# Two transformer blocks in one fp32 kernel: earlier loads of the down weights, and a new order of the activation sums' low parts

## The reference, cut to what matters

```
def swiglu_ffn(x, w_gu, w_down):            # first block, layers 0 and 1
    g, u = jnp.split(x @ w_gu, 2, axis=-1)
    return (jax.nn.silu(g) * u) @ w_down

def conv_ffn(h, w_gate, w_up, conv_w, conv_b, w_down):   # second block
    g = causal_dwconv(h @ w_gate, conv_w, conv_b)        # 3 taps along the tokens
    return (jax.nn.silu(g) * (h @ w_up)) @ w_down
```

## Time and profile before

| what | value |
|---|---|
| median of 3 runs | 2450.75 us (2448.09 to 2450.96) |
| the profiled execution's own time | 2450.39 us |
| its span, first to last instruction | 2448.6 us |
| PE busy | 2371.0 us (97%) |
| DVE busy | 1603.1 us (65%) |
| ACT busy | 1044.6 us (43%) |
| mean granted PE clock | 0.987 of full speed |
| chain that ended last | PE 86%, DVE 7%, ACT 3%, issue 2%, DMA 1% |

### The profile page before, as it was taken

The page is one execution under the profiler, slowest core; times in us unless marked ns, Lnnn a source line. Parts: engine busy times, 40 slices in busy tenths (PEclk is TensorE's granted clock), DMA queues, the critical chain, the costliest instruction groups (busy, mean ns, idle before and its releaser), DMA issues.

```text
span 2448.6 us, 36911 instructions
## 1 busy us (share of the span) xinstructions
PE 2371.0 (97%) x14899; PEld 2057.2 (84%) x14899; DVE 1603.1 (65%) x2174; ACT 1044.6 (43%) x1385; POOL 320.0 (13%) x258
## 2 busy tenths in 40 slices
PE   7699999999999999999999999999899999999899
PEld 7688899988886789998878669899788878899887
DVE  8835877835537678775675646899534545789832
ACT  5422544523226544444233644456322344355622
POOL 6403000003003240000232021000131002000000
PEclk9899999999999999999999999999999999999999
DMA  2423333333232133323333213232332312333232
GB/s 57 96 99 102 88 104 104 93 90 104 94 104 56 40 103 88 106 83 94 95 95 111 69 35 104 78 108 66 109 100 88 98 58 70 90 108 105 84 86 90
DMA packets 328204, 217.57 MB, mean 89 GB/s; under 512 B 11060, under 2 KB 318922, under 8 KB 327978
## 3 DMA queue, kind: packets, MB, share of 16 engines
q1 hardware_dynamic: 322298, 208.46, 29.1%
q0 software_dynamic: 2384, 5.80, 1.0%
q10 hardware_dynamic: 3360, 1.02, 0.2%
HBM read 206.59 MB, written 2.10 MB: 85 GB/s over the span
## 4 chain that ended last, share of the span: by engine, by line
PE 86%; DVE 7%; ACT 3%; issue 2%; DMA 1%; SPq 1%; ACTq 0%; POOL 0%; DVEq 0%
PE psum L1339 9%; PE psum L1341 9%; PE psum L1340 9%; PE psum L1095 8%; PE psum L1097 8%; PE psum L1096 8%; PE psum L1308 3%; PE psum L1309 3%; PE psum L1310 3%; PE psum L1477 2%; PE psum L1479 2%; PE psum L1478 2%; DVE w_lo L2918 1%; DMA w_stage<-in_ffn_w_down_dram 1%; PE psum L1207 1%
## 5 line engine op out<-in xcount | busy, mean ns | idle before, releaser
L2028 ACT CAST w_hi<-w_stage 128x2048 fp32r<-128x2048 f32 x129 | 246.6, 1912 | 720.9 <-PE psum L1097 409.8
L2918 DVE TENSOR_TENSOR w_lo<-w_stage,w_hi 128x2048 fp32r<-128x2048 f32 x126 | 298.7, 2371 | 287.3 <-ACT w_hi L2028 287.2
L1339 PE MATMUL psum<-x_sum_hi,w_hi 128*128 128x256 f32 x1088 | 310.0, 285 | 7.3 <-DVE hidden_raw L2975 7.3
L1340 PE MATMUL psum<-x_sum_lo,w_hi 128*128 128x256 f32 x1088 | 309.5, 285 | 0.0
L1341 PE MATMUL psum<-x_sum_hi,w_lo 128*128 128x256 f32 x1088 | 309.5, 285 | 0.0
L2096 ACT CAST w_hi<-w_parts 128x1024 fp32r<-128x1024 f32 x204 | 213.0, 1048 | 192.3 <-PE psum L1341 111.2
L3046 DVE TENSOR_TENSOR w_lo<-w_parts,w_hi 128x1024 fp32r<-128x1024 f32 x204 | 248.4, 1220 | 57.0 <-ACT w_hi L2096 55.9
L1339 PE MATMUL psum<-x_hi,w_hi 128*128 128x256 f32 x816 | 231.5, 284 | 0.0
L1341 PE MATMUL psum<-x_hi,w_lo 128*128 128x256 f32 x816 | 231.4, 284 | 0.0
L1340 PE MATMUL psum<-x_lo,w_hi 128*128 128x256 f32 x816 | 231.4, 284 | 0.0
L1095 PE MATMUL psum<-hidden_raw_hi,w_hi 128*128 128x512 f32 x572 | 224.0, 392 | 1.4 <-DVE w_lo L2918 1.4
(11 more groups left out here) (586 smaller groups left out, 5330.2 us busy)
## 6 DMA issues: line engine op xcount, KB each, us to landing
w_stage<-in_ffn_w_down_dram SPq DMA_DIRECT2D x64, 704.0 KB, 4.6
w_parts<-in_ffn_w_gu_dram SPq DMA_DIRECT2D x144, 256.0 KB, 3.5
w_parts<-in_ffn_w_gate_dram SPq DMA_DIRECT2D x64, 256.0 KB, 3.1
w_parts<-in_ffn_w_up_dram SPq DMA_DIRECT2D x64, 256.0 KB, 3.0
w_stage<-in_sb_w_qkv_dram SPq DMA_DIRECT2D x12, 1024.0 KB, 5.2
w_stage<-in_od_w_in_dram SPq DMA_DIRECT2D x12, 1024.0 KB, 5.3
w_stage<-in_ev_w_in_dram SPq DMA_DIRECT2D x10, 1024.0 KB, 5.1
w_stage<-in_ssm_w_glu_dram SPq DMA_DIRECT2D x8, 1024.0 KB, 5.4
```

The costliest lines, as they stand in the source:

```text
L1339: nc.tensor.matmul(dst, hi, x_hi[:, k, :], start=(start and k == 0), stop=False, skip_group_check=True)
L1340: nc.tensor.matmul(dst, hi, x_lo[:, k, :], start=False, stop=False, skip_group_check=True)
L2028: nc.scalar.copy(whi[:, half, :], wst[:, half, :]).then_inc(whi_done, 1)
L2918: V.tensor_tensor(wlo[:, half, :], wst[:, half, :], whi[:, half, :].bitcast(F32), ALU.subtract).then_inc(wlo_done, 1)
```

## The change

Three things are changed. (1) On SP the first down weights and the rest of each half are loaded half by half: half 0 after product 3 of the last iteration, half 1 after product 7; the down loop then begins with its second column block (`first`). (2) The low parts of the activation sums get a semaphore of their own, `x_low`; PE no longer waits for all four at the start, and each product that uses a sum waits for as many as it needs. To have a semaphore for this, `gv_link` is dropped and `rstds_done` counts in its place. (3) In the conv stages DVE makes the low parts of T1 and T2 before the first seven-product iteration and those of T3 and T4, with the sums of four, inside it; the taps come ahead of the sums of two; ACT rounds T2 between the first and second activations of the last plain iteration. In the gu stages two of the four low parts trade places.

```diff
@@ SP, part_loads and the loop over stages
-                sp.wait_ge(product_done, products_count(name, SEVEN_ITERS[name] - 1, 9))
+                down = run[run.index(name) + 1]
                 for half in range(2):
+                    sp.wait_ge(product_done, products_count(name, SEVEN_ITERS[name] - 1, 3 + 4 * half))
+                    sp.dma_start(tile_view(wst, down, half), tile_source(down, 0, half)).then_inc(w_landed[half], 16)
                     sp.dma_start(wst[:, half, DOWN_K * P:].rearrange("p (k n) -> p k n", n=P),
                                  down_rest(name)).then_inc(parts_landed[half], 16)
...
-                first = 1 if st.it0 == 0 else 0
+                first = 1 if st.it0 == 0 or run[run.index(name) - 1] in SEVEN else 0
@@ PE, seven_products (also for t2, t3, t4 with x_low_count 2, 3, 4)
-                pe.wait_ge(low_ready, rounded_count(name, 0, 0))
...
-                        pe.wait_ge(low_ready, rounded_count(name, i, tile + 1))
+                        pe.wait_ge(low_ready, low_count(name, i, tile + 1))
...
+                        pe.wait_ge(x_low, x_low_count(name, 1))
                         product(z_half(tile), i, 2 * tile, *t1, True)
@@ ACT, seven_gate_stage
-                for n, made in ((2, 3), (3, 7), (0, 10), (1, 12)) if conv else ((0, 1), (2, 2), (1, 3), (3, 4)):
-                    round_sum(n, made)
-                plain_gates(plain - 1)
+                if conv:
+                    for n, made in ((2, 3), (3, 7), (0, 10)):
+                        round_sum(n, made)
+                    plain_gates(plain - 1, lambda: round_sum(1, 12))
+                else:
+                    for n, made in ((0, 1), (2, 2), (1, 3), (3, 4)):
+                        round_sum(n, made)
+                    plain_gates(plain - 1)
@@ DVE, start, conv_start and conv_iteration
-                    for n, count in ((0, 1), (2, 2), (1, 3), (3, 4)):
+                    for n, count in ((0, 1), (1, 3), (2, 2), (3, 4)):
...
-                    for n, count in ((2, 1), (3, 2), (0, 3), (1, 4)):
-                        x_sum_low(n, count)
+                    x_sum_low(0, 3)
+                    for u in range(2):
+                        taps(4 + u, u, bank[u])
+                    x_sum_low(1, 4)
                     for tile in range(2):
                         sums_of_two(0, tile)
-                    for u in range(2):
-                        taps(4 + u, u, bank[u])
                     low_pair(0, 0, 0)
+                    plain_hidden(2, 0)
+                    low_pair(0, 0, 1)
                     for tile in range(2):
                         sum_of_three(0, tile)
-                    plain_hidden(2, 0)
-                    low_pair(0, 0, 1)
                     plain_hidden(2, 1)
-                    for tile in range(2):
-                        sum_of_four(0, tile)
                     low_pair(0, 1, 0)
...
                         hidden_first(i - 1)
                         hidden_second(i - 1)
+                    else:
+                        for tile in range(2):
+                            sum_of_four(0, tile)
+                        x_sum_low(2, 1)
                     low_pair(i, 2, 0)
+                    if i == 0:
+                        x_sum_low(3, 2)
```

More of the change, by code:

```diff
@@ L417, in build_blocks @@
         summed, rounded, low_ready = sem("summed"), sem("rounded"), sem("low_ready")
-        product_done, copied, added = sem("product_done"), sem("copied"), sem("added")
+        product_done, copied, added, x_low = sem("product_done"), sem("copied"), sem("added"), sem("x_low")
         block = ctx.enter_context(nc.Block())
@@ L507, in rounded_count, with low_count, x_low_count @@
             return list(SEVEN).index(name) * 4 + (before(name) + i) * 8 + 4 + n
+        def low_count(name, i, n):
+            return (before(name) + i) * 8 + n
+        def x_low_count(name, n):
+            return list(SEVEN).index(name) * 4 + n
         def summed_count(name, i, n):
@@ L585, in tile_source @@
                 rows = w.rearrange("(k p) n -> p k n", p=P)[:, half * DOWN_K:(half + 1) * DOWN_K]
-                return rows[:, :, bass.ds(i * P, P)]
+                return rows[:, :, bass.ds(i * P + first * P, P)]
             w, col = {
@@ L661, in part_loads @@
                         if i > 1:
-                            sp.wait_ge(low_ready, rounded_count(name, i - 2, 6 + tile + 1))
+                            sp.wait_ge(low_ready, low_count(name, i - 2, 6 + tile + 1))
                         load(i, tile, A21, 1, 0, parts_landed[tile])
@@ L666, in part_loads @@
                         if i > 0:
-                            sp.wait_ge(low_ready, rounded_count(name, i - 1, tile + 1))
+                            sp.wait_ge(low_ready, low_count(name, i - 1, tile + 1))
                             sp.wait_ge(summed, summed_count(name, i - 1, 2 + tile + 1))
@@ L1363, in seven_products @@
                     for tile in range(2):
-                        pe.wait_ge(low_ready, rounded_count(name, i, 2 + tile + 1))
+                        pe.wait_ge(low_ready, low_count(name, i, 2 + tile + 1))
                         pe.wait_ge(copied, copied_count(name, i, 2 * tile + 2))
+                        pe.wait_ge(x_low, x_low_count(name, 2))
                         product(x_of[tile], i, 4 + 2 * tile, *t2, False)
@@ L1368, in seven_products @@
                     for tile in range(2):
-                        pe.wait_ge(low_ready, rounded_count(name, i, 4 + tile + 1))
+                        pe.wait_ge(low_ready, low_count(name, i, 4 + tile + 1))
                         pe.wait_ge(added, added_count(name, i, tile + 1))
+                        pe.wait_ge(x_low, x_low_count(name, 3))
                         product(x_of[tile], i, 8 + 2 * tile, *t3, False)
@@ L1373, in seven_products @@
                     for tile in range(2):
-                        pe.wait_ge(low_ready, rounded_count(name, i, 6 + tile + 1))
+                        pe.wait_ge(low_ready, low_count(name, i, 6 + tile + 1))
                         pe.wait_ge(added, added_count(name, i, 2 + tile + 1))
+                        pe.wait_ge(x_low, x_low_count(name, 4))
                         product(x_of[tile], i, 12 + tile, *t4, False)
@@ L2061, in seven_gate_stage, with plain_gates @@
                 layer = int(name[-1])
-                def plain_gates(i):
+                def plain_gates(i, between=None):
                     for u in range(2):
@@ L2071, in plain_gates @@
                             nc.scalar.activation(tmp_a[:, u, :], bank[u][:, :], ACT.Silu).then_inc(act_out, 1)
+                    if between is not None:
+                        between()
                     if conv:
@@ L2154, in hidden_high @@
                         if c == 0:
-                            act.wait_ge(low_ready, rounded_count(name, end, 2 + 2))
+                            act.wait_ge(low_ready, low_count(name, end, 2 + 2))
                             act.wait_ge(summed, summed_count(name, end, 4 + 2))
                         if c == 7:
-                            act.wait_ge(low_ready, rounded_count(name, end, 4 + 1))
+                            act.wait_ge(low_ready, low_count(name, end, 4 + 1))
                         if c == 1:
-                            act.wait_ge(low_ready, rounded_count(name, end, 6 + 2))
+                            act.wait_ge(low_ready, low_count(name, end, 6 + 2))
                         if c == 18:
```

18 lines of the change are left out of this document (9 added, 9 removed).

## The result

The changed kernel takes **2421.51 us** (median of 4 runs, 2421.17 to 2421.82) against 2450.86 for the kernel before (median of 4, 2448.09 to 2452.52): ratio 0.9881, 95% interval 0.9864 to 0.9898. It is 29 us faster, where 36 were forecast, and 0.5 us outside the range.

The account below looks back on a forecast made before the run. PE bounds the kernel (busy 97%), so only its idle or low-clock stretches can yield time. 17.3 + 9.2 + 7.0 + 2.9 = 36.4 us off 2450.4 gives 2414.0, predicted as 2414.5 us; range 2410 to 2421.

Parts of the forecast that it names:

- Idle at the down restarts: PE's waits at the first matmul of four down stages, shortened by loading down weights by half: 17.3 us saved.
- The gu terms: Down restarts after gu0 and gu1: PE idle falls to 0.3 us, saving 3.7 and 4.15 us.
- the conv terms: Down restarts after conv0 and conv1: PE idle falls to 1.9 us, saving 4.5 and 5.0 us.
- The clock at the down restarts: PE no longer restarts at 1.2 GHz: 2.6 and 2.4 us in gu stages, 2.2 + 2.0 in conv, sum 9.2.
- clock falls in the conv gaps: Rival: the 1.9 us conv gaps still lower PE's clock; 2416.5 us with one, 2418.7 with both; chance 0.22.
- The conv start: First seven-product matmul of each conv stage: less DVE work ahead removes PE's 3.5 us wait, 7.0 us in all.
- its clock term of 2.9 us: Low clock behind the two conv starts' waits disappears: 1.4 us each, 2.9 us.
- the slack of 0.6 us: First conv iteration: DVE's 21.6 us of work lets the first seed run 0.6 us before product 9 needs it.
- the DMA wait is gone: Down restarts: loads issued after products 3 and 7 land by about 466 and 472 us, so casts don't wait.
- Free edits: Exchange of two gu low parts, dropped semaphore and 272 added x_low waits on PE cost 0 us.
- The rival's price of 0.15 us: Rival: each of 272 third waits on PE costs 0.15 us, giving 2455.3 us; chance 0.04 for any such cost.
- The prediction's row of one idle us with clock 1.00: A profile window with PE 0.15 busy and clock 1.00, used to assume that 1.9 us conv gaps keep the clock.

Follow-up runs that it names:

- run 1: Changed kernel with the conv down stages' first matmul no longer waiting for the second gate's Silu: 2414.24 us, ratio 0.986.
- run 2: Kernel before the change, with only the wait for the second gate's Silu dropped at the conv down stages: 2446.61 us, ratio 0.9988.
- run 4: Kernel before the change, with only the new early SP loads of the down weights: 2434.25 us, ratio 0.9933.
- run 5: Kernel before the change, loads still behind product 9, but the two 704 KB down loads ahead of the two of 320 KB: 2432.51 us, ratio 0.993.
- run 8: Changed kernel with three already met waits ahead of six more products of every iteration, 612 waits more: 2421.07 us, ratio 0.9891.
- run 9: Changed kernel with the low parts of T3 and T4 back ahead of the conv stages' first seven-product matmul, taps early: 2422.48 us, ratio 0.9894.
- run 10: Changed kernel with taps and T2's rounding back in their old places, low parts of T3 and T4 still inside the iteration: 2424.57 us, ratio 0.99.
- run 7: Run 1 plus first down half's cast and low part put first at conv ends, loads back behind product 9, 704 KB first: 2414.12 us, ratio 0.9859.
- run 3: Changed kernel with 14 small unused products on PE behind each conv stage's last seven-product matmul: 2418.39 us, ratio 0.987.

## Why the prediction was wrong, point by point

**The step that failed** is the reading of the earlier trace rows: "The name 'tmp_a L2148' that the list gives for the conv waits is only the ACT instruction that ended last before PE moved; DVE's low part (L3093) is the real releaser". The low part ended at 1722.17 and PE moved at 1724.42, 2.25 us later. In `gu0` the same hand-over took 0.10 us. The kernel before has the missing wait in its trace:

```profile
1722.09 0.74 DVE L2966 SCALAR_TENSOR_TENSOR tmp_a<-psum,params,tmp_a 128x511 f32<-128x511 f32 x1
...
1722.87 0.75 DVE L2969 SCALAR_TENSOR_TENSOR tmp_a<-psum,params,tmp_a 128x510 f32<-128x510 f32 x1
...
1723.65 0.72 ACT L2148 ACTIVATE tmp_a<-tmp_a,params 128x512 f32<-128x512 f32 x1 [1.52 <-DVE tmp_a L2969]
```

Two taps and a Silu, 0.78 + 0.78 + 0.72 us, end at 1724.37, and PE moves 0.05 us later. In the code it is the wait on `act_out` in `down_stage`, for all gate activations. Runs 1 and 2 show it directly: without it PE starts at the low part's end, and run 1 takes 2414.24 us, against 2414.5 forecast. That they are so near is in part luck, as run 1 still lost 1.7 us to the clock in `conv1`.

**Idle at the down restarts.** Forecast 17.3 us, measured 3.62 in `gu0`, 4.22 in `gu1`, 6.42 - 3.98 = 2.44 and 6.88 - 3.99 = 2.89 in the conv stages, 13.2 in all. The gu terms (3.7 and 4.15) were right, the conv terms (4.5 and 5.0) too large by 2.1 each, the length of the Silu's chain. The arithmetic for the low part was right: run 1 has 1.83 us for its 1.9.

**The clock at the down restarts.** Forecast 9.2 us, measured 2.6 + 2.4 in the gu stages, 2.2 - 1.7 = 0.5 in `conv0`, 2.0 - 2.5 = -0.5 in `conv1`, 5.0 in all. This is the rival "clock falls in the conv gaps", given 0.22, come true in both stages, with gaps of 4 us in place of 1.9. All twelve such gaps (4.0 to 4.6 us, two each in after and in runs 4, 5, 8, 9 and 10) had a mean clock of 0.75 to 0.85 behind them. At 1.9 us the chance was probably too low as well: in run 1 one of two such gaps was answered by the lower clock. Two gaps are few to price it by.

**The conv start.** Idle 7.0 us as forecast, no wait of PE left, and PEclk 1.00 behind it. The kernel after at `conv0`:

```profile
1527.28 1.23 DVE L3039 TENSOR_TENSOR x_sum_lo<-x_sum,x_sum_hi 128x1024 fp32r<-128x1024 f32 x1
...
1535.99 0.69 DVE L2995 TENSOR_TENSOR hidden_raw<-psum,tmp_a 128x512 f32<-128x512 f32 x1
...
1538.22 0.28 PE L1349 MATMUL psum<-x_sum_hi,w_hi 128*128 128x256 f32 x1
...
1548.77 0.43 DVE L3079 TENSOR_TENSOR psum<-psum,z_kept 128x256 f32<-128x256 f32 x1
```

DVE's work up to the first hidden values took 9.4 us, as forecast, and ended 1.5 us before PE needed it (1.6 forecast). The taps ended 5.7 us earlier in it than before and not 4, which changes nothing. That its clock term of 2.9 us belongs to this part depends on the execution: in run 4 the gap of `conv0` cost none and that of `conv1` 2.9 us by its window, the same sum in another way. Inside the first conv iteration nothing is late: the first `seed` ran 21.5 us after DVE's start, against 21.6 forecast, and ended at 1549.20, 0.5 us before product 9 was due (1538.22 + 8 x 1.44 = 1549.74). PE has no wait there, so the slack of 0.6 us held. In run 10, where DVE waits 1.64 us for ACT, it is used up.

**The loads.** They land in time, as forecast, though one reading was loose: at 477.94 us only the first half's load had to be there, not all four. But "the DMA wait is gone" was not the whole of it: run 5 shows that, as long as the Silu is awaited, the order of the loads alone does as much, and run 7 that their earliness pays only with the two later waits gone.

**Free edits.** The third wait costs nothing, and 612 more waits don't either. The rival's price of 0.15 us runs from the end of `hidden_raw` in the earlier trace rows and not from a low part's.

**The sum.** 13.2 + 5.0 + 7.0 + 2.9 = 28.1 us, against 27.7 by the rest of the span and 28.6 by the whole, whose first 300 us happened to be 0.9 shorter. The forecast's 36.4 is above that by 4.1 us of idle and 4.2 us of clock, both behind the one wait. Faster, given 0.96, came; the range ended 0.5 us too low, because it took in the clock rival with the forecast gap and not a longer gap.

## What to carry to other kernels

When the view names a releaser and you hold another for the real one, compare the hand-over time with the same hand-over elsewhere: 2.25 us in one place and 0.10 in another pointed here to a second wait in between. A restart can have as many waits in a row as it has semaphores, and an edit is worth only the distance to the next one, so price the next one too, down to the last; an edit that is worth nothing today can be worth 5 us after the next. Look also for where a wait went: in run 10 the same 0.7 us stands in the same line of the list as in run 9, but 12.5 us further on. Where an idle gap remains, its clock cost is a chance and not a number: it belongs in the range, at the window's full price.

## What the runs showed of the hardware

The clock's answer to a gap isn't set by the gap's length alone. Gaps of 1.83 us got 1.00 and 0.83 (run 1), gaps of 3.50 us 1.00 and 0.71 (run 4), gaps of 3.98 and 3.99 us 0.83 and 0.75 (after), in the mean over the next 10 us. The Trainium skill, page "TensorE: Matmul & The Clock Gate", Part 1, says that the activity watch is free-running; these pairs agree with that. The gaps of 4 us and more were all answered by a lower clock. When PE was kept at work with small matmuls for 3.29 us of such a gap and idle for 0.86, the mean was 1.00 both times (run 3).

The clock can also fall when PE is already at work again. In run 1, `conv1`, PE restarted at 2281.97:

```profile
2280.97:2281.97 1.00, 0.00 (x0) 0.03 (x1) 1.00 (x2) 0.85 (x2) 0.00 (x0) 1.00 0.00 0
2281.97:2282.97 1.00, 0.99 (x3) 0.86 (x4) 0.96 (x2) 0.00 (x0) 0.00 (x0) 0.67 0.00 0
2282.97:2283.97 1.00, 1.00 (x4) 0.72 (x4) 1.00 (x3) 0.62 (x1) 0.00 (x0) 0.50 0.45 126
...
2285.97:2286.97 1.00, 1.00 (x6) 0.83 (x5) 1.00 (x2) 1.00 (x3) 0.00 (x0) 1.00 0.09 26
```

It is at 2.4 GHz through the whole gap, falls to 1.2 GHz within the first us of work (mean 0.67), and is back at 2.4 GHz 4 us after the restart. The clock inside the gap alone would have made it seem harmless. The prediction's row of one idle us with clock 1.00 was such a row, and weak evidence; there the clock did stay at 1.00 in the 10 us behind it too.
